# A transformer block pair with a mixture of experts: mixture head and tail by tile, first layer modulated by 256 features, norm order in two layers, context projected under the second layer's end

## What is computed

```
u = layer_norm(x) * (1 + sc1) + sh1
proj = u @ w_in + b_in            # 2560 columns for four mixers, 4 for a forget gate, 4096 for gates
merged = sum_n sigmoid(gate_n) * (branch_n @ w_branch[n])     # pool, short conv, two attentions
x = layer_norm(ALPHA * x + g1 * (merged @ w_o)) * ln1_g + ln1_b
u2 = layer_norm(x) * (1 + sc2) + sh2
x = layer_norm(ALPHA * x + g2 * (relu(u2 @ w_up + b_up)**2 @ w_down)) * ln2_g + ln2_b
```

```
h = x * (1 + sc2) + sh2
scores = softmax(h @ router_w); sel = scores + router_bias, in 4 groups of 4 experts
group = argmax of (sum of its two largest sel); experts = the two largest sel in it
f = sum over the two experts of weight * ((silu(h @ w_gate[e]) * (h @ w_up[e])) @ w_down[e])
x = layer_norm(ALPHA * x + g2 * f) * ln_g + ln_b
```

## Time and profile before

| | us |
|---|---|
| median of 3 runs | 2588.53 (2588.47 to 2595.26) |
| the profiled execution | 2594.92 |
| its span, first to last instruction | 2592.9 |
| PE busy | 2373.5 (92%) |
| DVE busy | 915.5 (35%) |
| ACT busy | 359.9 (14%) |
| transfers | 700.90 MB, mean 270 GB/s |

### The profile page before, as it was taken

One profiled execution on the slowest core, in us unless ns is written; L12 is line 12 of the kernel. 1 busy time (PEld: TensorE's weight loads), 2 busy tenths in 40 slices (PEclk: granted clock), 3 DMA queues, 4 the chain that ended last, 5 costly groups with the idle time before them and its releaser, 6 DMA issues.

```text
span 2592.9 us, 26363 instructions
## 1 busy us (share of the span) xinstructions
PE 2373.5 (92%) x10600; PEld 1417.9 (55%) x10600; DVE 915.5 (35%) x1991; ACT 359.9 (14%) x712; POOL 31.5 (1%) x54
## 2 busy tenths in 40 slices
PE   4999999989899999989997998898889979988986
PEld 4878698448678686456653333333367533333332
DVE  4244555444544455142544111111145531111113
ACT  1111111001121110000351111111100011111111
POOL 1000000002000000000000000000000000000000
PEclk9999999989899999989997999999989979999998
DMA  9444877736257587541042999999864249999995
GB/s 366 174 147 173 313 254 283 290 130 220 89 183 271 217 319 276 210 146 49 1 171 106 404 429 429 429 428 428 365 248 181 107 178 410 428 428 428 428 429 247
DMA packets 156723, 700.90 MB, mean 270 GB/s; under 512 B 5984, under 2 KB 7264, under 8 KB 131040
## 3 DMA queue, kind: packets, MB, share of 16 engines
q1 hardware_dynamic: 154064, 690.30, 67.5%
q0 software_dynamic: 2304, 8.39, 0.9%
q10 hardware_dynamic: 272, 1.05, 0.1%
HBM read 694.47 MB, written 5.24 MB: 270 GB/s over the span
## 4 chain that ended last, share of the span: by engine, by line
PE 72%; DMA 19%; DVE 4%; ACT 2%; SPq 1%; issue 1%; DVEq 0%; ACTq 0%
PE banks L604 71%; DMA ring<-in_exp_w_down_dram 18%; DMA ring<-in_w_in_dram 1%; SPq L2510 1%; DVE bn L1698 1%; DVE X L1719 0%; DVE X L1722 0%; ACT arena L1506 0%; PE banks L730 0%; SPq L2442 0%; DMA XN<-in_ctx_dram 0%; DVE arena L2067 0%; ACT arena L1478 0%; ACT arena L1358 0%; ACT UT L1320 0%
## 5 line engine op out<-in xcount | busy, mean ns | idle before, releaser
L604 PE MATMUL banks<-ring,arena 128*64 128x512 f32 (+3 forms) x3840 | 992.6, 589 | 75.6 <-DMA ring<-in_exp_w_down_dram 26.4
L604 PE MATMUL banks<-UT,ring 128*128 128x256 f32 (+1 forms) x3568 | 725.8, 362 | 9.0 <-DMA ring<-in_w_in_dram 4.3
L604 PEld LDWEIGHTS banks<-ring,arena 128*64 128x64 f32 (+1 forms) x3840 | 369.8, 148 | 664.3 <-issue 618.0
L604 PEld LDWEIGHTS banks<-UT,ring 128*128 128x128 f32 x3568 | 617.7, 192 | 93.7 <-issue 20.2
L2066 DVE TENSOR_TENSOR arena<-arena,banks 128x512 f32<-128x512 f32 x32 | 34.0, 1063 | 662.2 <-PE banks L604 662.2
L1648 DVE SCALAR_TENSOR_TENSOR acc<-ring,cact,acc 128x512 f32<-128x512 f32 x304 | 230.8, 759 | 10.8
L1478 ACT ACTIVATE arena<-banks 128x512 f32<-128x512 f32 (+1 forms) x128 | 84.4, 659 | 803.5 <-PE banks L604 764.4
L604 PE MATMUL banks<-arena 64*128 64x512 f32 (+5 forms) x768 | 149.6, 439 | 6.0 <-ACT arena L1358 3.2
L604 PEld LDWEIGHTS banks<-arena 64*128 64x128 f32 (+2 forms) x768 | 72.8, 173 | 85.1 <-issue 69.2
L604 PE MATMUL banks<-arena,ring 128*128 128x256 f32 x336 | 83.4, 379 | 0.0
L604 PEld LDWEIGHTS banks<-const,acc 128*128 128x128 f32 x432 | 66.3, 222 | 21.8 <-issue 12.6
(11 more groups left out here) (232 smaller groups left out, 1334.3 us busy)
## 6 DMA issues: line engine op xcount, KB each, us to landing
ring<-in_exp_w_gate_dram SPq DMA_DIRECT2D x64, 2048.0 KB, 22.2
ring<-in_exp_w_up_dram SPq DMA_DIRECT2D x64, 2048.0 KB, 25.3
ring<-in_exp_w_down_dram SPq DMA_DIRECT2D x64, 2048.0 KB, 17.1
ring<-in_w_in_dram SPq DMA_DIRECT2D x26, 2048.0 KB, 14.1
ring<-in_w_ada_dram SPq DMA_DIRECT2D x24, 2048.0 KB, 9.2
ring<-in_mod_w_dram SPq DMA_DIRECT2D x24, 2048.0 KB, 8.2
ring<-in_w_up_dram SPq DMA_DIRECT2D x16, 2048.0 KB, 8.0
ring<-in_w_down_dram SPq DMA_DIRECT2D x16, 2048.0 KB, 8.1
```

The source lines that it names most:

```text
L604: return nc.tensor.matmul(o, lhs, rhs, start=start, stop=stop)
```

## The change

1. **Start.** The four first steps are regrouped: each w_ada piece now carries 256 shift and 256 scale columns, so each gives a quarter of the features. The first two w_in pieces stand between them in the ring. Banks are zeroed, and pieces 0 and 1 are multiplied in parts of two feature blocks as the quarters come. The other constants are asked for before w_in piece 2.
2. **finish_tiles** takes a half's statistics right after the half; in layers 0 and 1 the seventh modulation step beside w_down stands between tile 0 and tile 1 (DVE) and behind the last piece (PE).
3. **Context**: a ring piece, turned under w_down of layer 1, modulated by ACT by tile, its key and value products ahead of the turn of X; pieces in order 2, 3, 4, 0, 1; window keys copied early; rotation scratch in `acc`.
4. **Mixture head**: attn_w_out products reordered; gate rows first; turn, modulate and route by tile; sums zeroed behind the router; ranks by one broadcast compare; count and flag behind the one-hot.
5. **Mixture loop and tail**: DVE empties down times the gate (`gsplit`); the sums go from the banks straight onto ALPHA x; `mixture_read` comes from the first last scatter; the output is stored by tile.
6. **Hyena**: the output product waits for each channel alone.

```diff
@@ plan_pieces
     for n in range(FIRST_STEPS):
-        out.append(("ada",) + MOD_STEPS[n][:2])
+        out.append(("ada", 0, n))
+        if n < 2:
+            out.append(("in", 0, n))
...
+            if (l, j) == (1, 5):
+                out.append(("ctx", 0, 0))
             add("dn", l, j)
...
-            out += [("ain", 0, j) for j in range(5)] + [("hyc", 0, 0), ("wo", 2, 0), ("wo", 2, 1), ("ffo", 0, 0)]
+            out += [("ain", 0, j) for j in (2, 3, 4, 0, 1)] + [("wo", 2, 0), ("wo", 2, 1), ("ffo", 0, 0), ("hyc", 0, 0)]
@@ tensor engine, block_one
-                    modulation(FIRST_STEPS)
-                    turn_evicted(("u", l))
-                    pe.wait_ge(rest_loaded, 16 * NREST)
...
+                        for c in range(2):
+                            for k in (2 * n, 2 * n + 1):
+                                x = mm(held[g][:, c * N:c * N + N], w[:, k, col + c * P:col + c * P + P], UT[:, k, :],
+                                       False, k + c == KC)
...
+                    for g in groups:
+                        held[g] = take(pe, g)
+                        mm(held[g], zero, C("ones", 0, 1).to_broadcast([P, 512]), True, False)
+                    first_modulation(0)
+                    for i in (0, 1):
+                        part(0, i)
+                    first_modulation(1)
+                    for n, i in ((1, 0), (1, 1), (0, 2), (0, 3), (1, 2), (1, 3)):
+                        part(n, i)
+                    first_modulation(2)
+                    for i in range(3):
+                        part(2, i)
+                    first_modulation(3)
+                    part(2, 3)
+                    for i in range(4):
+                        part(3, i)
...
+                if l == 1:
+                    rows = piece(pe, ("ctx", 0, 0))[:, 0:TT * D].rearrange("p (t d) -> p t d", d=D)
+                    for t in range(TT):
+                        turn_tile(("hc", 2), rows, t, hold=t == 1)
+                    release(("ctx", 0, 0), (("hc", 2), 1, 1))
                 for j in range(DOWN_BOTH, 8):
-                    if j == 7:
-                        beside("dn", l, 6)
-                        if l == 0:
-                            turn_tile(("u", 1), XN, 0, xn_ready, 5)
+                    if j == 7 and l == 0:
+                        turn_tile(("u", 1), XN, 0, xn_ready, 5)
                     down_piece(j, (1,))
                 release(("dn", l, 7), names[-1])
+                beside("dn", l, 6)
@@ tensor engine, mixture
+                gate_rows(L, 1)
                 g = ("router", L)
...
+                    turn_tile(("m", L), X, t, x_ready, 4 * L + t + 1, by4=True)
...
+                        if k % 4 == 0:
+                            wait_evicted(pe, (("m", L), t, k // 4))
...
-                gate_rows(L, 1)
+                while group_n[0] % BANKS != 4:
+                    group_n[0] += 1
+                pe.wait_ge(zeros_ready, L - 1)
+                for n in range(4):
+                    pe.wait_ge(evicted[n], group_uses[n])
+                    mm(banks[:, n, :], SW[:, 0:P], YS, True, False)
@@ tensor engine, attention_block (end)
-                product(1, 1, range(0, 6))
                 wait_evicted(pe, ("o", 2, 1, 1))
-                for t in range(TT):
-                    for hf in range(2):
-                        product(t, hf, range(6, 8))
+                product(0, 0, range(6, 8))
+                product(0, 1, range(6, 8))
+                product(1, 0, range(6, 8))
+                product(1, 1, range(0, 8))
@@ scalar engine
+            def first_quarter(n):
+                wait_evicted(act, ("ada", 0, n, "x"))
+                k = 2 * n
+                A(UT[:, k, :], UT[:, k, :], ACT.Identity, bias=modc[:, 0, k:k + 1], scale=modc[:, 0, 8 + k:9 + k])\
+                    .then_inc(quarter_ready, 1)
...
+                    for n in range(FIRST_STEPS):
+                        if n:
+                            first_share(n)
+                        first_quarter(n)
...
+            def mixture_input(L):
+                norm_std(0)
+                modulate_tile(("m", L), L, 24, 0, (0, 1))
+                norm_std(1)
+                modulate_tile(("m", L), L, 24, 1, (0,))
...
+                    if L >= 2 and i == 1:
+                        own = slice(h * CAP, h * CAP + CAP)
+                        A(gsplit[own, :], bank[own, :], ACT.Copy)
...
-                        evict("down", e, YS)
@@ vector engine, finish_tiles
+                        if hf == 0:
+                            half_stats(t, 0)
+                    norm_affine(t, k, halves=(1,))
...
+                    if t == 0 and between is not None:
+                        between()
@@ vector engine, router
-                rank(four(rk), v, four(tm))
+                V.tensor_tensor(GT, other, this, ALU.is_gt)
+                link(V.tensor_tensor(EQ, other, this, ALU.is_equal))
+                link(V.tensor_tensor(EQ, EQ, low, ALU.mult))
+                link(V.tensor_tensor(GT, GT, EQ, ALU.add))
+                link(V.tensor_reduce(ranks, GT, AX.X, ALU.add))
@@ vector engine, mixture
                         done(V.tensor_tensor(XE, XE, sh, ALU.add), "turned")
+                        done(V.tensor_tensor(YS, start("down", e), gsplit, ALU.mult), "down")
...
-                        x = V.tensor_tensor(ACC[:, t, sl], banks[:, n, :], grow[:, sl], ALU.mult)
+                        x = V.scalar_tensor_tensor(out=xs, in0=xs, scalar=ALPHA, in1=banks[:, n, :],
+                                                   op0=ALU.mult, op1=ALU.add)
@@ sync
-            sp.wait_ge(x_ready, 16)
-            sp.dma_start(out.rearrange("b (t p) d -> p (b t) d", p=P), X[:, :, :]).then_inc(stored, 16)
+            for t in range(TT):
+                sp.wait_ge(x_ready, 15 + t)
+                sp.dma_start(out.rearrange("b (t p) d -> p (b t) d", p=P)[:, t, :], X[:, t, :]).then_inc(stored, 16)
```

452 lines of the change are left out of this document (257 added, 195 removed).

## The result

| | before | after |
|---|---|---|
| median, same chip, 4 runs each | 2591.48 (2588.47 to 2595.26) | 2518.2 (2516.46 to 2519.02) |
| the profiled execution | 2594.92 | 2518.36 |
| its span | 2592.9 | 2516.3 |
| PE busy | 2373.5 (92%) | 2358.8 (94%) |

The ratio is 0.9715 (95% interval 0.970 to 0.9729). The prediction was 2514.5 with a range of 2502 to 2532. The profiled executions are 76.6 us apart; the sum of the prediction was 75.6. PE's busy time fell by 14.7 us with eight more matmul instructions to do: that part is work at half clock that went; the other 62 us are waiting. The profiled execution of the kernel before lies 3.4 us above its median and that of the kernel after 0.2, so the medians are 73.3 apart where the profiles are 76.6 apart.

A forecast was written before the change was run, and what follows sets the result against it. Transfers were taken to bound the expert loops, a nearly always busy TensorE the rest. Gains summed to 75.6 us; off the 2588.5 median that gave 2513, with a likely new wait 2514.5 (range 2502 to 2532).

The forecast's parts named there:

- A: Start: first two w_in pieces used by quarters between modulation pieces; the chain, not transfers, sets the end; 8.7 us gained.
- B: End of layer 0: tile 0 finished before the modulation step, so TensorE's wait and slow clock go; 13.0 us gained.
- F: Mixture tails: sums straight from the banks, 0.8 us less for tile 0, 2.0 for tile 1; twice, 4.0.
- C: Layer 1 to attention: context turned early, its products before X, keys copied early; waits and slow clock go; 19 us.
- D: First mixture head: first part, logits by tile 7.1 us earlier; second part, ranks, zero fill and position product, 8.8; together 15.9.
- E: Second mixture head: logits 3.1 us earlier, same second part 8.8, output product channel by channel 1.83; together 13.7.
- R1: Rival: the start gains nothing because of cross waits and slowly run parts; 2523 us, chance 0.10.
- R2: Rival: the heads' gains are hidden because expert transfers set the expert loop; 2542 us, chance 0.06.
- R3: Rival: layer 1 to attention gains only 9 us instead of 19, something being late; 2524 us, chance 0.12.
- R4: Rival: working by tile in the heads does not come about, their first parts give nothing; 2525 us, chance 0.08.
- R6: Rival: the exponential's table load behind the gate rows is late, 0.5 us in each head; 2515.5 us, chance 0.04.
- R5: Rival: slower than before, DVE's down eviction delaying each expert's gate product beyond 3 us of slack; 2610 us, chance 0.02.

The follow-up runs named there:

- e1: Kernel after, with layer 0's last modulation step and its column sum back ahead of tile 0: median 2531.81 us, 13.6 more.
- e2: Kernel after, with X turned ahead of the context's key and value products instead of behind them: median 2523.69 us, 5.5 more.
- e3: Kernel after, with the ranks as 26 small DVE operations again: median 2527.11 us, 8.9 more.
- e4: Kernel after, with the zero fill of the four banks back just before the expert loop: median 2522.09 us, 3.9 more.
- e7: Kernel after, with eight idle TensorE products in the wait for the second quarter at the start: median 2519.34 us, 1.1 more.
- r9: Kernel after, with e8's heads, five idle products at the start, and layer 1's convolution, forget sums and rotations earlier on DVE: median 2499.28 us.
- e5: Kernel after, with two more unused DVE products ahead of each expert's down eviction: median 2544.84 us, 26.6 more.
- e6: Kernel after, with five more unused DVE products ahead of each expert's down eviction: median 2635.56 us, 117.4 more.
- r11: r10 without the idle products behind the first loop, keeping those in the heads: median 2494.78 us, 23.4 less than the kernel after.
- r12: e5 with two idle TensorE products in the wait ahead of each gate product: median 2527.04 us, 17.8 less than e5.
- e8: Kernel after, with each mixture's tile 0 turned ahead of the gate rows and the exponential ahead of their copies: median 2515.02 us, 3.2 less.
- r10: r9 with idle TensorE products in the waits of both mixture heads and behind the first loop: median 2497.03 us.

## Why the prediction was right, point by point

- **What bounds.** Right: transfers for the experts, TensorE and its waits for all else (the chain that ended last is now TensorE 74%, transfers 19%). Each term of the sum is found in its own stage within 1.3 us. That the sum of the profiled pair is off by only 1.0 has luck in it: A fell short by 1.3 and the score loop lost 1.2 that nobody had named, while B to F brought 3.5 more than forecast. The waits that e1, e2, e3 and e4 bring back are shown by experiment. The context's new place, the early copies of the keys, the new order at the start and the tails were not undone; for them the trace shows that the waits are gone, and no run takes the edit alone.
- **The base.** The 3.7 us between 2514.5 and 2518.2 are 3.0 of base: the median of before was 2588.53 in three runs and 2591.48 in four, because its executions lie near 2588 and near 2595. The sum was read in one of the longer executions, 2594.92, and taken off a median of three. By medians the gain was 73.3, where 74 had been forecast with the 1.5 allowed for a new wait. The 1.2 lost in the score loop come near that allowance by chance: they are no wait but a lower clock, 0.97 granted over 68 us instead of 1.00.
- **A, 8.7 against 7.4.** The times of the chain's steps were within 1.2 us. "The chain, not the transfers, sets the end" holds only from 27.3 us on: until then the chain that ended last is the transfer of the second w_ada piece, which landed 1.3 later than the 26 taken, and the last quarters hang on it. Mis-sized was the term "six parts of 8 instructions (10.4, with a slow start 12)": they took 13.43, after a wait of 4.43. e7 and r9 show the same instructions at 10.63.
- **B, 13.0 against 13.1.** e1 gives it back alone: 13.4.
- **C, 19 against 19.8.** All four waits went, with the slow stretches behind them. The order alone is 6.15 of it (e2). The copied keys were not undone by themselves; their 2.29 and the slow gate rows are gone from the trace. What is left are waits of 0.29 and 0.45 for DVE; the kernel before had one of 0.31 at the same place, so 0.4 is new where 0.7 was allowed for the rotations.
- **D, first part, 7.1 against 7.3**, with each step in place: root of tile 1 queued behind ACT's modulations (1.66), turn at 1.98.
- **D, second part, 8.8 against 9.1** (16.4 less 7.3). From product end to gate product it is 26.3, and 1.7 of slow start come on top: 28.0 where the sign said 28 to 29. The ranks took 2.1 (2.2 taken). The fill ended 5.4 behind the logits (5.3). e3 shows that beyond 0.7 of slack longer ranks are felt, and that the wait costs clock besides; e4 shows that the fill's place is worth 2 to 3.4 a head. The slow start of the loop, 1.7, was there. **E**: 13.7 against 14.2 by the same walk.
- **F, 2.0 against 2.75 a tail.** The four sums took 2.48, and the old form 2.61 + 0.24 + 1.23 + 1.22, with gaps 5.4. The term "2.0 for tile 1" was mis-subtracted: it is 2.9 less 0.1 for the eviction. The store by tile gave 1.4 (1.3 forecast).
- **Rivals.** R1 fell: from 36 to 67 us TensorE waits only 0.95 and 0.85. R2 fell: the 18 us that the first head won are still there at the last down product but for the slow start (16.4), and the first five down products follow each other at 27.25 us and wait for no transfer. R3 and R4 fell by C and D. R6: the table was loaded at 1350.03, the exponential ran at 1352.20 and waited for DVE, 0.89; covered. By the Trainium skill (ScalarE: Activation LUTs, What ACT_TABLE_LOAD costs) a drain of about 1.38 on top of the load would have made it late, by estimate at 1352.7. The trace does not agree: at 85.26 ACT starts a load 0.02 behind an ACTIVATE, it takes 1.28, and the next ACTIVATE starts at 86.55, 0.01 behind it.
- **R5 was priced wrongly, though it was right not to fear it.** The eviction on DVE costs little more than on ACT, a wait of 0.97 against 0.87. But the slack is 2.1 us, not 3: the prediction took TensorE's busy time of 26.4, and the wait for the down eviction, which is no work but is not slack either, comes on top (27.25). And a wait of 2.2 in front of the gate product already costs the clock. The step that failed is "It must pass 3 + 75/32 = 5.3 us each". Between e5 (1.2 of wait, 26.6) and e6 (3.0, 117.4) the 75 us of the change are used up at some 2.2 us of added wait, an estimate by straight line.

## What to carry to other kernels

In a kernel bound by TensorE price each wait twice: its length, and the clock behind it. Here waits of 2 to 10 us cost another 1.4 to 3 us of half-speed work, one of 1 us in the expert loop cost none, and an edit that shortens a wait gains both. Idle products in a wait give the clock back if they fit into it (r9, r11, r12); where they are too long (e7) or run slowly themselves (second head of r12), they cost more than they bring. Before trusting slack under a transfer, ask what a longer wait does to the period itself. And read an experiment in its rows, and only in those of the stage that was edited: in e3 and e4 the total fitted the rival and the rows the theory, and e8's span promised r9 3 us more in the heads than it got.

## What the runs showed of the hardware that I had not expected

- **The clock in a loop.** With waits of 0.97, 0.80 and 1.19 in an expert the gate and up products stayed at full clock behind the first expert. With one wait of 2.17 they lost 1.70 in 10 of the first loop's 16 (e5; granted clock 0.58 in their first 4 us). With one of 3.97 they lost 1.6 and 2.75 by turns (e6). Two idle products in the wait of 2.17 restore the clock (r12).
- **Sixteen-column products mostly ran at the clock that they found.** They were slow behind a wait and stayed so (granted clock 0.50; 3.60 in the kernel after), and ran at 1.96 where TensorE had been fed before (r10, r11). But in four first heads the clock fell between two rows of eight with 0.27 us idle between them (1.04, then 1.89, in e4).
- **Idle products stood still once.** The 4.03 us marked "issue" in r10 came amid 11 of them, while six transfers of weights were under way. One trace shows it; what holds the instructions back stays open.
- **Chance steps of the clock.** The same instructions of the score loop took 81.0 us in e2 and r9, 82.2 in the kernel after and 83.8 in r10 from the first gate rows to the next ones near its end, although no edit touches them. The first gate product of a loop took 13.95, 15.65 or 16.68 behind the same wait of 1.97. Single executions of one kernel differ by 3 to 12 us. Effects under some 5 us can't be read from a median of four here.
